# Sequence states read over four 32-column blocks, 96 places for the token tile, and quarters of the first weights, in a decoder trunk on one core

## The chip, the core and the metric

The kernel runs on one core of one Trainium2 chip. The metric is the device time of one execution in microseconds; the median of several runs is compared. One execution is also profiled, and its own time stands beside its span. A core has a matrix engine (TensorE, PE in the rows, with its weight loads as PEld), three engines for elementwise work (VectorE or DVE, ScalarE or ACT, GpSimd or POOL) and a queue that issues DMAs (SyncE or SP).

## The reference

Two layers of a decoder trunk. Each has a feed-forward part, a token mixer and a second feed-forward part. The mixer runs a gated delta rule in four heads (width 128) beside a short gated convolution. Two groups of tokens share the weights: one prompt (16 meta tokens and 256 tokens) and eight sequences of eight sampled tokens, each with a stored 128x128 state per head. What the change touches:

```python
def gdn_chunks(q, k, v, beta, g, s0, chunk):
    ...
    def step(s, inp):
        qd, kt, uc, wc, qkc, el = inp
        nv = uc - jnp.einsum('bhlk,bhkv->bhlv', wc, s)
        o = jnp.einsum('bhlk,bhkv->bhlv', qd, s) + jnp.einsum('bhij,bhjv->bhiv', qkc, nv)
        s = el[..., None, None] * s + jnp.einsum('bhlk,bhlv->bhkv', kt, nv)
        return s, o
```

For the eight sequences there is one chunk of eight tokens. So each sequence and head needs its stored state `s0` multiplied with its eight q columns (for `o`) and its eight k columns (for `nv`). The mean-square norms, the convolutions and the projections are as in any such trunk. Inputs and outputs are fp32.

## The kernel before

**Layout.** Features lie on the 128 partitions, tokens in the free dimension: 256 prompt tokens, then 64 sampled and 16 meta tokens, 336 in all (320 at the end, where the meta tokens are no longer needed). The mixer works on three token tiles; tiles 0 and 1 are the prompt's, tile 2 (`C_TILE`) holds the 64 sampled and the 16 meta tokens, 80 of its 128 places.

**Large products.** Weights come as fp32 in chunks of 512 KB halves (slots `RAW0` to `RAW2`), two halves to a chunk in the feed-forward entry: gate and up. ScalarE rounds a half to `WH`, VectorE makes the rest `WL = RAW - WH` in place; activations are split in the same way into `XH` and `XL`. One product of a tile is then three matmuls (`WH XH`, `WH XL`, `WL XH`) of 128x128 by 336.

**Start.** `entry` of layer 0 first runs 14 warm-up matmuls on zeros, then gate for the input tiles kt 0 to 3, up for the same, both for kt 4 to 7, and then the second chunk's two tiles one after the other. The SP queue issues x and the halves in the order that the rows of the change's section show.

**Mixer.** A hand-written list `BEHIND_PART` says which small steps stand behind each third of an input projection tile (`part`, six to nine large matmuls). All engines walk through the same list, each doing its piece of a step and waiting on semaphores for the pieces of others. Steps named in `EVACUATED_BY` are numbered; each writes one of three PSUM banks (5 + number mod 3) in turn, and `bank_free` on TensorE waits until the step three before has been read out. The steps near the change: `qk`, `kk` (products of keys with queries and keys), `unit`, `nt`, `x`, `y`, `mirror` (a triangular inverse by doubling, in 32x32 blocks, on MB, NB, XM and EGB), `vt`, `kt` (transposes of values and keys), `kst` (transpose of the keys times states), `nv`, `st`, `oC`, `o`, `o_cols`, `rob` (the recurrence's products and the output's norm).

**Reads.** `read` steps 0 to 7 (line 1912) multiply the stored states: per head and sequence the 128x128 state is the stationary side, and 16 columns, eight of q and eight of k, move. Four such matmuls make a step. The result stands in bank 3 (`READ_QK`), with features on the partitions; after read 7 ScalarE copies the k part to `KST`, which `kst` turns.

## Time and profile before

| | us |
|---|---|
| median of 3 runs | 1404.74 (1404.52 to 1405.12) |
| profiled execution | 1401.58 |
| its span | 1399.8 |
| TensorE busy | 1379.2 (99%) |
| VectorE busy | 860.7 (61%) |
| ScalarE busy | 638.7 (46%) |
| GpSimd busy | 30.8 (2%) |
| mean granted TensorE clock | 0.995 of full |

The page's sections give busy time by engine, the span in 40 slices, the DMA queues, the chain that ended last, and the costliest groups. In the rows further down, a line of the time order has the start in us, the length in us, engine, line, operation, output<-inputs, the size of the stationary side (rows\*columns) for TensorE, the size of the moving side, and a count; in square brackets the idle time before it and what ended it. An fp32 matmul shows as two records. A record's length runs to the end of its result, so the pace of a queue is read from start to start.

### The profile page before, as it was taken

Reading aid. Unit: us, or ns where it says so; the run is one execution under the profiler, and the core shown is the slowest. Engines: PE = TensorE matmul, PEld = TensorE weight load, DVE = VectorE, ACT = ScalarE, POOL = GpSimd, SP = SyncE. Lnnn points to the kernel's source line nnn. Section 1 sums busy time; section 2 is a strip of 40 time slices with the busy share of each in tenths; the row PEclk is TensorE's granted clock in tenths of the full one; section 3 lists DMA queues with packets and bytes.
Section 4 is the critical chain, followed back from the end, with each engine's and each line's share of the span. In section 5 each row is a group of like instructions: output and inputs, shape, how many; then the busy total and the mean of one; then the engine's idle time right before and its main releaser. Section 6 shows DMA issues by size and latency. Waiting matters only on the chain.

```text
span 1399.8 us, 25130 instructions
## 1 busy us (share of the span) xinstructions
PE 1379.2 (99%) x10704; PEld 1355.8 (97%) x10704; DVE 860.7 (61%) x1527; ACT 638.7 (46%) x1021; POOL 30.8 (2%) x129
## 2 busy tenths in 40 slices
PE   9999999999999999999999999999999999999997
PEld 9999999989999999999999999999899999999997
DVE  5655533798696765553376555337976968555433
ACT  5433333583635543433354443336826355444331
POOL 0000000110000000000000000001100000000000
PEclk9999999999999999999999999999999999999998
DMA  6644344422125344434435443444221263444342
GB/s 211 221 151 138 117 143 145 149 93 93 67 77 203 121 151 144 133 121 146 164 131 194 144 150 123 144 138 139 91 98 61 91 219 121 151 151 151 125 145 100
DMA packets 49760, 190.93 MB, mean 136 GB/s; under 512 B 6160, under 2 KB 8720, under 8 KB 49136
## 3 DMA queue, kind: packets, MB, share of 16 engines
q1 hardware_dynamic: 49040, 184.19, 39.1%
q0 software_dynamic: 608, 5.12, 0.9%
q8 instruction: 85, 1.39, 0.4%
q14 instruction: 27, 0.22, 0.0%
HBM read 182.86 MB, written 6.43 MB: 135 GB/s over the span
## 4 chain that ended last, share of the span: by engine, by line
PE 92%; DVE 4%; ACT 3%; issue 1%; DMA 0%; SPq 0%; ACTq 0%
PE PS L1552 26%; PE PS L1553 26%; PE PS L1554 26%; PE PS L1592 2%; PE PS L1597 2%; PE PS L1593 2%; PE PS L1758 2%; DVE WL L1077 1%; PE PS L1912 1%; DVE CV L1239 1%; PE PS L1756 1%; PE PS L1887 1%; PE PS L1868 0%; PE PS L1979 0%; ACT WH L746 0%
## 5 line engine op out<-in xcount | busy, mean ns | idle before, releaser
L1552 PE MATMUL PS<-XH,WH 128*128 128x336 f32 (+1 forms) x1728 | 549.8, 318 | 0.3 <-DVE WL L1077 0.3
L1554 PE MATMUL PS<-XH,WL 128*128 128x336 f32 (+1 forms) x1728 | 542.9, 314 | 0.0
L1553 PE MATMUL PS<-XL,WH 128*128 128x336 f32 (+1 forms) x1728 | 542.6, 314 | 0.0
L1077 DVE TENSOR_TENSOR WL<-RAW,WH 128x1024 fp32r<-128x1024 f32 (+1 forms) x312 | 398.7, 1301 | 193.7 <-ACT WH L746 193.3
L746 ACT ACTIVATE WH<-RAW 128x1024 fp32r<-128x1024 f32 (+1 forms) x312 | 343.9, 1120 | 226.9 <-DMA RAW<-in_w_down 170.9
L1552 PEld LDWEIGHTS PS<-XH,WH 128*128 128x128 f32 x1728 | 325.1, 188 | 4.2 <-issue 3.1
L1553 PEld LDWEIGHTS PS<-XL,WH 128*128 128x128 f32 x1728 | 325.2, 188 | 0.4
L1554 PEld LDWEIGHTS PS<-XH,WL 128*128 128x128 f32 x1728 | 324.9, 188 | 0.0
L1552 PE MATMUL PS<-HH,WH 128*128 128x336 f32 (+1 forms) x704 | 221.4, 314 | 0.0
L1553 PE MATMUL PS<-HL,WH 128*128 128x336 f32 (+1 forms) x704 | 221.3, 314 | 0.0
L1554 PE MATMUL PS<-HH,WL 128*128 128x336 f32 (+1 forms) x704 | 221.2, 314 | 0.0
L1201 DVE TENSOR_TENSOR GR<-PS,RB 128x336 f32<-128x336 f32 (+1 forms) x88 | 44.2, 503 | 186.4 <-PE PS L1554 186.3
L841 ACT ACTIVATE HH<-HF 128x336 fp32r<-128x336 f32 (+1 forms) x88 | 42.6, 484 | 203.1 <-DVE HF L1209 203.1
L1552 PEld LDWEIGHTS PS<-HH,WH 128*128 128x128 f32 x704 | 132.6, 188 | 0.0
L1553 PEld LDWEIGHTS PS<-HL,WH 128*128 128x128 f32 x704 | 132.2, 188 | 0.0
L1554 PEld LDWEIGHTS PS<-HH,WL 128*128 128x128 f32 x704 | 132.1, 188 | 0.0
L839 ACT ACTIVATE SG<-GR 128x336 f32<-128x336 f32 (+1 forms) x88 | 42.4, 482 | 114.5 <-DVE GR L1201 114.5
L1211 DVE TENSOR_TENSOR HL<-HF,HH 128x336 fp32r<-128x336 f32 (+1 forms) x88 | 44.4, 505 | 48.4 <-ACT HH L841 48.4
L1592 PE MATMUL PS<-XH,WH 128*128 128x336 f32 (+1 forms) x177 | 57.1, 326 | 1.9 <-DVE WL L1077 1.9
L1593 PE MATMUL PS<-XH,WL 128*128 128x336 f32 (+1 forms) x177 | 55.6, 318 | 0.0
L1239 DVE SCALAR_TENSOR_TENSOR CV<-EXT,PAR_ALL,CV 128x360 f32<-128x360 f32 x72 | 42.6, 591 | 4.9 <-ACT CV L876 3.2
L1597 PE MATMUL PS<-XL,WH 128*128 128x336 f32 (+1 forms) x177 | 45.3, 319 | 0.0
(283 smaller groups left out, 1222.0 us busy)
## 6 DMA issues: line engine op xcount, KB each, us to landing
RAW<-in_w_up SPq DMA_DIRECT2D x176, 512.0 KB, 4.3
RAW<-in_w_down SPq DMA_DIRECT2D x64, 704.0 KB, 4.1
RAW<-in_w_in SPq DMA_DIRECT2D x56, 512.0 KB, 4.4
RAW<-in_w_out SPq DMA_DIRECT2D x16, 512.0 KB, 4.4
SEQ_S<-in_states SPq DMA_DIRECT2D x2, 2048.0 KB, 10.7
out_state_s<-SEQ_S POOLq DMA_DIRECT2D x2, 2048.0 KB, 8.9
X<-in_x SPq DMA_DIRECT2D x8, 168.0 KB, 5.1
out_y<-X SPq DMA_DIRECT2D x4, 320.0 KB, 2.3
```

The source lines that it names most:

```text
L746: act.activation(WH[slot][:, cols], RAW[slot][:, cols], ACT.Copy).then_inc(split_hi.sem, 1)
L841: act.activation(hidden(HH, c, n), HF[k][:, 0:n], ACT.Copy).then_inc(h_hi.sem, 1)
L1077: dve.tensor_tensor(WL[slot][:, cols], RAW[slot][:, cols], WH[slot][:, cols].bitcast(F32), ALU.subtract).then_inc(split_lo.sem, 1)
L1201: dve.tensor_tensor(GR[k][:, 0:n], PS[:, up_bank(c, 0), 0:n], RB[:, 0:n], ALU.mult).then_inc(gate_scaled.sem, 1)
L1211: dve.tensor_tensor(hidden(HL, c, n), HF[k][:, 0:n], hidden(HH, c, n).bitcast(F32), ALU.subtract).then_inc(h_lo.sem, 1)
L1239: ins = dve.scalar_tensor_tensor(cv, src[:, n, tap:tap + length - taps + 1], PAR_ALL[:, layer, col:col + 1], cv, ALU.mult, ALU.add)
L1552: pe.matmul(out, wh, xh, start=first, stop=False)
L1553: pe.matmul(out, wh, xl, start=False, stop=False)
L1554: return pe.matmul(out, wl, xh, start=False, stop=last)
L1592: pe.matmul(out, wh, XH[:, kt, 0:n], start=(kt == 0), stop=False)
L1593: pe.matmul(out, wl, XH[:, kt, 0:n], start=False, stop=False)
L1597: ins = pe.matmul(out, wh, XL[:, kt, 0:n], start=False, stop=(kt == KT - 1))
```

## The change

Three edits.

1. **Reads.** The eight `read` steps of a layer go. GpSimd blanks a new tile `QKZ` (it shares its place with `TMP`) and, at step `qk` of tile 2, copies q and k of each sequence into it, in pairs of sequences with 16 zero columns between them. A new step `tread`, numbered and read out by ScalarE into `VS`, runs 32 matmuls: stationary side a window of 32 columns of `QKZ` (one sequence's 16 columns and 16 zeros), moving side the 128 columns of the state, output one of four 32-column blocks of the array. The two sequences of a pair add up in one block. One later step `read` multiplies the result with a 0/1 matrix `seq_order`, which puts it into `READ_QK` as before. VectorE's step for projection tiles c waits for the copy, since `TMP` shares its place with `QKZ`.
2. **96 places.** Steps of tile 2 work on 96 instead of 128 places (`C_SPAN`), `kst` on 64: fewer columns, and three instead of four 32x32 blocks.
3. **Quarters.** At the very start the first two chunks are loaded and split in quarters of 512 columns. The first quarters of all four tiles come first, and `entry` runs kt 0 to 3 of gate, up, gate2, up2, then kt 4 to 7 of gate and up, then of gate2 and up2. The squares of x on ScalarE stand behind all splits of these chunks.

```diff
+C_SPAN = 96
...
+PAIR_W = 6 * SEQ_T
...
-    [("read", 0), ("x", 0, 2), ("y", 2, 2), ("silu", 9)],
-    [("lo", 5, 1), ("mirror", 2, 2), ("read", 1), ("conv", 10), ("nt", 1), ("x", 2, 4)],
+    [("x", 0, 2), ("y", 2, 2), ("silu", 9)],
+    [("lo", 5, 1), ("mirror", 2, 2), ("conv", 10), ("nt", 1), ("x", 2, 4), ("tread",)],
...
+        tmp_at = region(max(2 * T, HEADS * SEQS // 2 * PAIR_W) * 4)
+        (TMP0, TMP1), _ = stack(tmp_at, ("TMP0", [P, T], F32), ("TMP1", [P, T], F32))
+        (QKZ,), _ = stack(tmp_at, ("QKZ", [P, HEADS, SEQS // 2, PAIR_W], F32))
+        TMP = [TMP0, TMP1]
...
+        def span_of(t):
+
+            return C_SPAN if t == C_TILE else P
+
+        def own_cols(t):
+
+            return slice(t * P, t * P + span_of(t))
...
+        def quarters(half):
+
+            return [slice(half * A_LEN // 2 + q * A_LEN // 4, half * A_LEN // 2 + (q + 1) * A_LEN // 4) for q in range(2)]
...
+            def load_quarter(c, half, q):
+
+                cols = quarters(half)[q]
+                ready = early_in[c][half] if q == 0 else raw_in[c][half].sem
+                sp.dma_start(RAW[c][:, cols], source(0, c)[:, cols]).then_inc(ready, 16)
+
             load_x(0)
-            load_half(0, 0, 0)
+            load_quarter(0, 0, 0)
             for m in range(1, 4):
                 load_x(m)
-            load_half(0, 0, 1)
-            for m in range(4, KT):
-                load_x(m)
-            load(0, 1)
+            load_quarter(0, 1, 0)
+            load_quarter(1, 0, 0)
+            load_quarter(1, 1, 0)
+            load_x(4)
+            load_x(5)
+            load_quarter(0, 0, 1)
+            load_quarter(0, 1, 1)
+            load_x(6)
+            load_x(7)
+            load_quarter(1, 0, 1)
+            load_quarter(1, 1, 1)
...
+                pool.memset(QKZ[:, :, :, :], 0.0).then_inc(qk_blank.sem, 1)
...
+                    elif what == "qk" and t == C_TILE:
+
+                        pool.wait_ge(q_decayed.sem, q_decayed.at(ORDER.index(C_TILE), layer))
+                        pool.wait_ge(qk_blank.sem, qk_blank.at(0, layer))
+                        for h in range(HEADS):
+                            for k in range(2):
+                                own = QKV[:, h + HEADS * k, N_PROMPT:N_PROMPT + N_SAMPLE].rearrange(
+                                    "p (a b i) -> p a b i", b=2, i=SEQ_T)
+                                for b in range(2):
+                                    at = 4 * SEQ_T * b + SEQ_T * k
+                                    ins = pool.tensor_copy(QKZ[:, h, :, at:at + SEQ_T], own[:, :, b, :])
+                        ins.then_inc(qk_spread.sem, 1)
...
-                    elif what == "read" and t == READS - 1:
+                    elif what == "tread":
+
+                        evacuated(act.activation(VS[:, C_TILE, :, :], group(step, layer), ACT.Copy))
+                    elif what == "read":
...
+                    act_group(("tread",), layer)
...
-                        dve.tensor_tensor(qT(tcols(t)), qT(tcols(t)), QKM[:, t, :, :], ALU.mult).then_inc(q_decayed.sem, 1)
+                        own_t, s = own_cols(t), span_of(t)
+                        dve.tensor_tensor(qT(own_t), qT(own_t), QKM[:, t, :, 0:s], ALU.mult).then_inc(q_decayed.sem, 1)
                         dve.wait_ge(q_decayed.sem, q_decayed.at(NTH[step], layer))
                         dve.wait_ge(dd_exp.sem, dd_exp.at(NTH[step], layer))
-                        evacuated(dve.tensor_tensor(QKM[:, t, :, :], group(step, layer), DA[:, t, :, :], ALU.mult))
+                        evacuated(dve.tensor_tensor(QKM[0:s, t, :, 0:s], group(step, layer)[0:s, :, 0:s], DA[0:s, t, :, 0:s],
+                                                    ALU.mult))
...
+            def early_low(n):
+
+                c, cols = n // 2, quarters(n % 2)[0]
+                dve.wait_ge(early_hi, n + 1)
+                dve.tensor_tensor(WL[c][:, cols], RAW[c][:, cols], WH[c][:, cols].bitcast(F32),
+                                  ALU.subtract).then_inc(early_lo, 1)
+
+            def rest_low(c, half):
+
+                cols = quarters(half)[1]
+                dve.wait_ge(split_hi.sem, split_hi.at(PIECE[c] + half, 0))
+                dve.tensor_tensor(WL[c][:, cols], RAW[c][:, cols], WH[c][:, cols].bitcast(F32),
+                                  ALU.subtract).then_inc(split_lo.sem, 1)
+
             prenorm(0, 0, 0)
-            split_low(0, 0, 0)
+            early_low(0)
             for m in range(1, 4):
                 prenorm(0, 0, m)
-            split_low(0, 0, 1)
-            for m in range(4, KT):
-                prenorm(0, 0, m)
-            split_low(0, 1, 0)
-            split_low(0, 1, 1)
+            for n in range(1, 4):
+                early_low(n)
+            prenorm(0, 0, 4)
+            prenorm(0, 0, 5)
+            rest_low(0, 0)
+            rest_low(0, 1)
+            prenorm(0, 0, 6)
+            prenorm(0, 0, 7)
+            rest_low(1, 0)
+            rest_low(1, 1)
...
-                    for kt in range(4):
-                        part(kt, gate)
+                    for n_early, tile in enumerate((gate, up, gate2, up2)):
+                        pe.wait_ge(early_lo, n_early + 1)
+                        for kt in range(4):
+                            part(kt, tile)
+                    split(layer, at, 0)
                     split(layer, at, 1)
-                    for kt in range(4):
-                        part(kt, up)
                     for kt in range(4, KT):
                         part(kt, gate, up)
-                    for tile in (gate2, up2):
-                        split(layer, at + 1, tile[1])
-                        for kt in range(KT):
-                            part(kt, tile)
+                    split(layer, at + 1, 0)
+                    split(layer, at + 1, 1)
+                    for kt in range(4, KT):
+                        part(kt, gate2, up2)
                     return
+                split(layer, at, 0)
...
-            def per_head_products(name, layer, lhsT, rhs, transpose=False):
+            def per_head_products(name, layer, lhsT, rhs, transpose=False, rows=P, cols=P):
                 bank_free(name, layer)
-                out = heads_bank(name)
+                out = heads_bank(name)[0:rows, :, 0:cols]
                 for h in range(HEADS):
                     if transpose:
-                        ins = pe.transpose(out[:, h, :], lhsT(h), mask("ident"))
+                        ins = pe.transpose(out[:, h, :], lhsT(h), mask("ident", cols)[0:cols])
...
-                                for b in range(P // SQUARE):
+                                for b in range(span_of(t) // SQUARE):
...
+                    elif what == "tread":
+
+                        pe.wait_ge(states_in.sem, states_in.at(0, layer))
+                        pe.wait_ge(qk_spread.sem, qk_spread.at(0, layer))
+                        bank_free(step, layer)
+                        out = heads_bank(step)
+                        for h in range(HEADS):
+                            for b in range(2):
+                                for pair in range(SEQS // 2):
+                                    window = QKZ[:, h, pair, 2 * SEQ_T * b:2 * SEQ_T * b + QUAD]
+                                    ins = pe.matmul(out[block(pair), h, :], window, SEQ_S[:, 2 * pair + b, h, :],
+                                                    start=(b == 0), stop=(b == 1))
+                        ins.then_inc(filled.sem, 1)
                     elif what == "read":
 
-                        h, half = t // 2, t % 2
-                        if t == 0:
-                            pe.wait_ge(states_in.sem, states_in.at(0, layer))
-
-                            pe.wait_ge(proj_read.sem, proj_read.at(3, layer))
-                            pe.wait_ge(q_decayed.sem, q_decayed.at(ORDER.index(C_TILE), layer))
-                        for s in range(half * SEQS // 2, (half + 1) * SEQS // 2):
-                            own = slice(s * SEQ_T, (s + 1) * SEQ_T)
-                            cols = slice(N_PROMPT + s * SEQ_T, N_PROMPT + (s + 1) * SEQ_T)
-                            ins = pe.matmul(READ_QK[:, h, :, own], SEQ_S[:, s, h, :], QKV[:, h:2 * HEADS:HEADS, cols],
-                                            start=(h == 0 and s == 0), stop=(h == HEADS - 1 and s == SEQS - 1))
-                        if t == READS - 1:
-                            ins.then_inc(seq_read.sem, 1)
+                        pe.wait_ge(proj_read.sem, proj_read.at(3, layer))
+                        evacuated(("tread",), layer)
+                        for h in range(HEADS):
+                            ins = pe.matmul(READ_QK[:, h, :, :], VS[:, C_TILE, h, :], mask("seq_order"), start=(h == 0), stop=(h == HEADS - 1))
+                        ins.then_inc(seq_read.sem, 1)
...
+    found["seq_order"] = (col % N_SAMPLE // SEQ_T == row // (2 * SEQ_T)) & (col // N_SAMPLE == row // SEQ_T % 2) & (col % SEQ_T == row % SEQ_T)
```

The same edit of `C_SPAN` is made in the other steps of tile 2.

TensorE around the first two reads, layer 0, before. NB, XM, EGB and MB are the inverse's tiles; L1552 to L1554 are the large matmuls:

```order
1965 L1554 MATMUL PS<-XH,WL_57 128x336
1966 L1912 MATMUL PS<-QKV,SEQ_S 128x2x8 x4
1967 L1868 MATMUL PS<-NB_110,DA 32x16 x16
1968 L1887 MATMUL PS<-EGB,MB_117 32x16 x16
1969 L1552 MATMUL PS<-XH,WH_58 128x336
...
1977 L1554 MATMUL PS<-XH,WL_55 128x336
1978 L1912 MATMUL PS<-QKV,SEQ_S 128x2x8 x4
1979 L1868 MATMUL PS<-NB_116,DA 32x16 x16
1980 L1552 MATMUL PS<-XH,WH_58 128x336
...
1988 L1554 MATMUL PS<-XH,WL_55 128x336
1989 L1887 MATMUL PS<-XM_79,MB_111 32x16 x16
1990 L1887 MATMUL PS<-EGB,MB_117 32x16 x16
```

And after (L1646 to L1648 are the large matmuls, L2008 is `tread`):

```order
1963 L1648 MATMUL PS<-XH,WL_57 128x336
1964 L1965 MATMUL PS<-NB_111,DA 32x16 x16
1965 L1984 MATMUL PS<-EGB,MB_118 32x16 x12
1966 L1646 MATMUL PS<-XH,WH_58 128x336
...
1974 L1648 MATMUL PS<-XH,WL_55 128x336
1975 L1965 MATMUL PS<-NB_117,DA 32x16 x12
1976 L2008 MATMUL PS<-SEQ_S,QKZ 32x128 x32
1977 L1646 MATMUL PS<-XH,WH_58 128x336
...
1985 L1648 MATMUL PS<-XH,WL_55 128x336
1986 L1984 MATMUL PS<-XM_79,MB_112 32x16 x16
1987 L1984 MATMUL PS<-EGB,MB_118 32x16 x12
```

Two reads of four matmuls went, the 32 matmuls of `tread` stand behind the third x step, and x and y of tile 2 have 12 matmuls. The order products (four of 128x128) stand where reads 3 and 4 stood.

The SP queue at the start, before (RAW_52 and RAW_53 are the first two chunks):

```order
1 L632 DMA PAR_ALL<-in_par 128x218
2 L630 DMA X<-in_x 128x336
3 L612 DMA RAW_52<-in_w_up 128x1024
4 L630 DMA X<-in_x 128x336 x3
5 L612 DMA RAW_52<-in_w_up 128x1024
6 L630 DMA X<-in_x 128x336 x4
7 L612 DMA RAW_53<-in_w_up 128x1024 x2
8 L641 DMA MK<-in_masks 128x256
```

After:

```order
1 L650 DMA PAR_ALL<-in_par 128x218
2 L648 DMA X<-in_x 128x336
3 L655 DMA RAW_52<-in_w_up 128x512
4 L648 DMA X<-in_x 128x336 x3
5 L655 DMA RAW_52<-in_w_up 128x512
6 L655 DMA RAW_53<-in_w_up 128x512 x2
7 L648 DMA X<-in_x 128x336 x2
8 L655 DMA RAW_52<-in_w_up 128x512 x2
9 L648 DMA X<-in_x 128x336 x2
10 L655 DMA RAW_53<-in_w_up 128x512 x2
11 L672 DMA MK<-in_masks 128x256
```

The first quarters of both chunks now stand ahead of x 4 to 7.

ScalarE at the start, before (L771 makes XH, L746 WH, L775 the squares):

```order
2 L771 ACTIVATE XH<-X,PAR_ALL 128x336
3 L746 ACTIVATE WH_58<-RAW_52 128x1024
4 L771 ACTIVATE XH<-X,PAR_ALL 128x336 x3
5 L746 ACTIVATE WH_58<-RAW_52 128x1024
6 L771 ACTIVATE XH<-X,PAR_ALL 128x336 x4
7 L775 ACTIVATE SQ_122<-X 128x336 x4
8 L746 ACTIVATE WH_59<-RAW_53 128x1024 x2
9 L775 ACTIVATE SQ_122<-X 128x336 x4
10 L746 ACTIVATE WH_60<-RAW_54 128x1024 x2
```

After:

```order
2 L815 ACTIVATE XH<-X,PAR_ALL 128x336
3 L1089 ACTIVATE WH_58<-RAW_52 128x512
4 L815 ACTIVATE XH<-X,PAR_ALL 128x336 x3
5 L1089 ACTIVATE WH_58<-RAW_52 128x512
6 L1089 ACTIVATE WH_59<-RAW_53 128x512 x2
7 L815 ACTIVATE XH<-X,PAR_ALL 128x336 x2
8 L1095 ACTIVATE WH_58<-RAW_52 128x512 x2
9 L815 ACTIVATE XH<-X,PAR_ALL 128x336 x2
10 L1095 ACTIVATE WH_59<-RAW_53 128x512 x2
11 L819 ACTIVATE SQ_123<-X 128x336 x8
```

Eight roundings of 512 columns stand in place of four of 1024, and all squares behind them.

## Rows read from the trace of the kernel before

**Rows 1.** Busy time by engine, from the page's first section.
```profile
PE 1379.2 (99%) x10704; PEld 1355.8 (97%) x10704; DVE 860.7 (61%) x1527; ACT 638.7 (46%) x1021; POOL 30.8 (2%) x129
```

**Rows 2.** The reads: their group (count, busy us, mean ns), then time order.
```profile
L1912 PE MATMUL PS<-QKV,SEQ_S 128*128 128x16 f32 x128 | 15.4, 255 | 0.0
...
330.79 0.96 PE L1912 MATMUL PS<-QKV,SEQ_S 128*128 128x16 f32 x8
331.68 0.44 PE L1868 MATMUL PS<-NB,DA 32*32 32x16 f32 x32
```

**Rows 3.** Time order, TensorE: small products over four blocks, and one weight load.
```profile
312.80 0.48 PE L1797 MATMUL PS<-SQX,MK 128*32 128x336 f32 x2
312.81 0.48 PE L1797 MATMUL PS<-SQY,MK 128*32 128x336 f32 x2
313.50 0.42 PE L1552 MATMUL PS<-XH,WH 128*128 128x336 f32 x1
...
312.84 0.12 PEld L1797 LDWEIGHTS PS<-SQY,MK 128*32 128x32 f32 x2
...
367.74 1.08 PE L1943 MATMUL PS<-VS,MB 32*32 32x128 f32 x32
368.75 0.42 PE L1552 MATMUL PS<-XH,WH 128*128 128x336 f32 x1
```

**Rows 4.** Time order, TensorE: eight products, x and y steps, transposes of keys.
```profile
315.32 1.95 PE L1758 MATMUL PS<-QKV 128*128 128x128 f32 x16
317.03 0.40 PE L1552 MATMUL PS<-XH,WH 128*128 128x336 f32 x1
...
335.72 0.44 PE L1868 MATMUL PS<-NB,DA 32*32 32x16 f32 x32
335.99 0.96 PE L1887 MATMUL PS<-XM,MB 32*32 32x16 f32 x64
...
364.38 0.60 PE L1756 MATMUL PS<-MK,KST 128*128 128x128 f32 x4
364.91 0.68 PE L1861 MATMUL PS<-N,DA 64*64 64x64 f32 x8
```

**Rows 5.** Time order of GpSimd, VectorE and ScalarE around the reads.
```profile
256.17 2.00 POOL L690 COPY EXT<-HIST_G 128x24 f32<-128x24 f32 x12
277.86 1.52 POOL L704 COPY NEW_G<-EXT 128x3 f32<-128x3 f32 x1 [7.30 <-DVE EXT L1260]
...
312.01 0.69 DVE L1363 TENSOR_TENSOR QKV<-QKV,QKM 128x512 f32<-128x512 f32 x1 [1.07 <-PE PS L1758]
...
329.81 0.21 DVE L1417 TENSOR_TENSOR NB<-NB,PS 128x64 f32<-128x64 f32 x1
...
333.14 0.42 ACT L894 ACTIVATE QKV<-CV 128x256 f32<-128x256 f32 x1 [16.30 <-DVE CV L1239]
```

**Rows 6.** Start in time order, then windows (busy of PE, PEld, DVE, ACT, POOL, PEclk).
```profile
1.07 6.04 PE L2016 MATMUL PS<-TMP 128*128 128x128 f32 x28 [1.07 <-DVE TMP L1515]
8.97 0.42 PE L1592 MATMUL PS<-XH,WH 128*128 128x336 f32 x1 [1.86 <-DVE WL L1077]
...
24.36 0.32 PE L1597 MATMUL PS<-XL,WH 128*128 128x336 f32 x1
25.43 0.32 PE L1552 MATMUL PS<-XH,WH 128*128 128x336 f32 x1
...
4.41 0.58 ACT L771 ACTIVATE XH<-X,PAR_ALL 128x336 fp32r<-128x336 f32 x1 [2.38 <-DMA X<-in_x]
6.60 1.06 ACT L746 ACTIVATE WH<-RAW 128x1024 fp32r<-128x1024 f32 x1 [1.61 <-DMA RAW<-in_w_up]
...
9.22 1.06 ACT L746 ACTIVATE WH<-RAW 128x1024 fp32r<-128x1024 f32 x1 [0.16 <-DMA RAW<-in_w_up]
...
10.00:12.00 2.00, 2.00 (x9) 1.78 (x8) 2.00 (x4) 2.00 (x5) 0.00 (x0) 0.52 1.05 385
...
376.00:378.00 2.00, 2.00 (x9) 2.00 (x8) 1.94 (x3) 1.98 (x3) 0.00 (x0) 0.50 0.00 0
```

133 lines of the change are left out of this document (78 added, 55 removed).

## The prediction

> **What bounds the kernel now.** I read the page first, then the matmul groups by form, then the order of time on TensorE, then VectorE, ScalarE and GpSimd at the same places. The page gives TensorE 1379.2 busy of 1399.8 us, 99%, against 61% for the next engine [rows 1]. The kernel's time is what stands in TensorE's queue, plus what it waits. So an edit is worth the time between the start of the removed instructions and the start of the next one. The two mixers hold the sequence reads: 128 records of 15.4 us together (two records are one fp32 matmul) [rows 2]. A read step of four matmuls stands at 330.79, and the next instruction at 331.68: 0.89 us for only 16 moving columns each [rows 2]. Four 128-column products cost nearly the same, eight of them 1.71 us [rows 4]. So a read is paid for its 128x128 stationary state, not for the columns that move. The profiled execution took 1401.58 us (span 1399.8), 3.2 us under the median of the timed runs, 1404.74. I take differences from the trace and subtract them from the median.
>
> **Reads (edit 1).** Removed per layer: 8 steps at 0.89, 7.1 us. Added per layer: 32 products with 32 stationary and 128 moving columns over four column blocks, two rounds of four per head, 8 rounds; then four 128x128 order products. Two rows come near to a round. Four products with 32 stationary columns, one in each block, with 336 moving ones, stand at 312.80 to 312.81, and the next instruction at 313.50: 0.70 us, so four run side by side; scaled to 128 columns 0.27. Sixteen 32x32 tiles with 128 moving columns go from 367.74 to 368.75, four rounds in 1.01, 0.25 each [rows 3]. Both carry a turn into the next instruction of about 0.1 us once. Eight rounds are then between 8 x 0.21 + 0.1 = 1.8 and 8 x 0.27 = 2.2; I take 1.9, nearer the second row, which has several rounds in a row as here. If the four blocks didn't share time, each product would cost what one of the eight in 1.71 us does, 0.21, and 32 of them 6.8 us: the far bound, against the 0.70 row. The order products are half of 1.71, 0.86 us [rows 4]. Three times a small step followed a read directly and now pays the turn itself, 0.2 us per layer together. Net: 7.1 - 1.9 - 0.86 - 0.2 = 4.15 per layer, **8.3 us** in all.
>
> A rule bears on the round. In the first of these two rows the last of the eight weight loads starts at 312.84, while the products of the first pass run [rows 3]. The Trainium skill, "TensorE: Matmul & The Clock Gate", section "The mechanism", says that a weight load overlaps a running matmul only where its row group is another one; all four column blocks share all rows. By that rule the loads would stand between the rounds; it is the first rival below. The 0.70 us row doesn't show such a gap, but holds only two passes.
>
> **What has to be ready for them.** GpSimd copies q and k into the padded tile, 16 small copies, after the decay of q at 312.01 (0.69 us). Like copies took 2.00 us for 12, 0.17 each [rows 5]: done by 315.5. The 32 products are due near 330.3 (the x step at 331.68, its 0.28, less the two reads ahead). Cover: 15 us. Behind these copies on GpSimd stand only history copies whose results leave by DMA at the end of the stage; the new memset of 768 elements goes into the seven us before 277.86 in which the engine waits [rows 5]. The 128x512 copy out of PSUM falls to ScalarE, whose queue then stands idle for 16.30 us until 333.14 [rows 5]; a copy of about 0.6 us from 332.2 is gone before that, and the x step that needs the bank comes two steps and one part later, near 334.2. The keys are copied to KST four parts earlier than now. Nothing here is on the path.
>
> What gets tighter is the x step behind the first y step. Its operand leaves VectorE at 329.81 to 330.02 [rows 5] and is used at 331.68 now; without the two reads it would be used near 330.0. VectorE gets some shorter operations ahead of it (96 instead of 128). From then on the 32 products (1.9) stand where two reads (1.8) stood, so the next ones keep their distance. Later each group loses 0.9 us at most against gaps of VectorE of 0.4 to 1 us. I charge **0.5 us** for such waits in all, bounds 0 and 2.
>
> **96 places (edit 2).** On TensorE per layer: qk and kk of the token tile, 8 products of 0.21 (1.71 / 8), go from 128 to 96 on both sides. Between nothing (a record costs 0.11 with 16 moving columns too) and a quarter, 0.43; I take 0.35, since here the stationary side shrinks too. Six x and y steps lose 4 of 16 small products; such a step is 0.27 (335.72 to 335.99) [rows 4], a quarter is 0.07: 0.4. nv keeps its four rounds, nothing. The rest 0.1. Together 0.85 per layer, **1.7 us**, bounds 0 and 2.2. Shorter operations on VectorE and ScalarE lie beside TensorE.
>
> The turned keys now fill 64 rows. Today four transposes take 0.53 us (364.38 to 364.91), under the 0.86 of four products [rows 4]. The Trainium skill, "TensorEngine Tiling (Array Packing)", section "Restrictions", says that column tiling switches off the transpose mode for fp32. If that befell this step, it would cost 0.3 us per layer more, 0.7 in all. No row shows a transpose of 64 columns, so I don't count it.
>
> **Quarters at the start (edit 3).** Now: x lands and is read at 4.41, the first half of the weights at 6.60, ScalarE takes 1.06, VectorE the 1.2 up to TensorE's start at 8.97; its warm-up products had ended at 7.11, an idle of 1.86 us. Then its granted clock falls: 0.52 of full speed in 10 to 12 us, nearly all of it at the lower level, 1.2 GHz. The entry ends at 25.43; the seven products before that take 1.07, 0.153 each [rows 6]. Ninety-six of them are 14.7, so 1.7 us of the 16.46 are the clock's and the turn's. New: the first quarter is 0.26 MB earlier in the queue than the half was. From 0.28 MB at 4.4 and 0.80 MB at 6.6 it lands at 5.5. ScalarE and VectorE need about 0.6 and 0.7 on 512 columns: ready at 6.9, and TensorE starts at 7.05, right behind its warm-up. Gate takes 12 products, to 9.0. The up quarter closes 1.32 MB; with 1.85 MB at 9.22 [rows 6] it lands at 7.9, and is split at about 9.4: a wait of 0.4. The other two are ready by 11, the second quarters by 13 to 15 against needs at 15 and 18.6. Then 84 products end at 22.4. Chunk 2 is split later than before (the squares now stand ahead of it, to about 20.4 on VectorE), but still before 22.4. That is 25.43 - 22.4 = **3.0 us**, 1.9 of it the earlier start and the rest the clock. Bounds: 0.5 (quarters that land late, clock still low) and 3.6.
>
> **Sum.** 8.3 + 1.7 + 3.0 - 0.5 = 12.5 us. 1404.74 - 12.5 = **1392.2**; the profiled execution would be near 1389.1, its span 1387.3.
>
> **Rivals.**
> *Loads between rounds.* Each of the 16 passes of a layer (8 rounds, two passes) waits for four loads of 32 columns. Four reads with eight 128-column loads took 0.89, 0.11 a load, so four of 32 columns are again 0.11: 16 x 0.11 = 1.7 per layer, 3.4 in all: 1395.6. For it: the blocks share rows. Against: 0.70 for two passes of 336.
> *The start gives nothing.* 2 KB pieces move more slowly, or the wait for the up quarter lets the clock fall all the same: 1395.2. For it: a gap of 1.86 did it. Against: the queue order, and that the new gap is 0.4.
> *The clock in the mixer.* Layer 0 has a stretch at the lower level (0.50 at 376 to 378 [rows 6]) behind a row of small-tile steps, of about the start's price, 1.7 us; layer 1 has none. With fewer busy tiles there may be none, one or two: -1.7 or +1.7 on the forecast.
> *The change doesn't do what it says.* The four blocks run one after another: reads 7.1 against 6.8 + 0.86: 8.3 turns into -1.5: 1402.
> *Slower: GpSimd's copies.* They decide from 1.1 us each (17.6 us from 312.7 to 330.3 over 16). One small copy there took 1.52 us [rows 5]. At that price 16 take 24.3 us: TensorE stands 6.7 us in each layer, and a gap over 1.86 us brings a low-clock stretch of 1.7: 2 x 8.4 = 16.8 on top: 1409. Against: that copy was the first of its line after a long rest, and twelve others took 0.17 each.
>
> **Chances.** Forecast with its clock variants 0.67, loads between rounds 0.12, no gain at the start 0.12, no sharing 0.04, copies 0.04, the rest 0.01. A measurement of this kernel can tell about 0.2%, 2.8 us, from no change. Faster by more 0.93, within 0.03, slower 0.04. Range: low end 1389.0 (forecast, start and 96 at their better bounds and no low clock in the mixer), high end 1397.5 (either of the first two rivals with a low-clock stretch more).
>
> **What would show it.** Right: the 32 products span under 2 us, the order products 0.86; TensorE's idle before its first product near 0.1, the granted clock 1.00 from 10 to 14 us, chunk 2's first product near 22.4; no wait of TensorE on GpSimd or on the bank. Wrong: 3.4 or 6.8 us for the 32 products, a clock of 0.5 before 20 us, or idle time before the third x step.

## The result

| | before | after |
|---|---|---|
| median of the first comparison, us | 1404.63 (1403.46 to 1405.12, 4 runs) | 1388.07 (1386.85 to 1390.4, 4 runs) |
| profiled execution, its span | 1401.58, 1399.8 | 1390.4, 1388.6 |
| all executions measured here, median | 1400.91 (1398.44 to 1406.25, 74, without the first series) | 1388.25 (1386.85 to 1391.13, 15, with the first series) |

The ratio of the first comparison is 0.9885, 95% interval 0.9868 to 0.9902: 16.6 us less, where 12.5 was forecast. The time lies 0.9 us below the range. Two later series of the same kernel, beside before on the same chip, gave 0.9911 (0.9896 to 0.9926) and 0.9908 (0.9892 to 0.9924), 12.4 and 12.7 us.

Busy time by engine, after, as in [rows 1]:

```profile
PE 1369.5 (99%) x10608; PEld 1344.1 (97%) x10608; DVE 859.2 (62%) x1529; ACT 638.6 (46%) x1027; POOL 38.1 (3%) x163
```

TensorE is busy 9.7 us less. Time order of TensorE after (start, length, engine, line, operation, count of records). The rows show, from the top, the first large product, the one that waits for up, chunk 2's first product, the token tile's products, the reads, the order products and the turned keys.

```profile
6.47 0.40 PE L1686 MATMUL PS<-XH,WH 128*128 128x336 f32 x1
...
9.41 0.42 PE L1686 MATMUL PS<-XH,WH 128*128 128x336 f32 x1 [0.46 <-DVE WL L1602]
...
22.40 0.32 PE L1646 MATMUL PS<-XH,WH 128*128 128x336 f32 x1
...
312.04 1.76 PE L1853 MATMUL PS<-QKV 128*96 128x96 f32 x16
313.55 0.40 PE L1646 MATMUL PS<-XH,WH 128*128 128x336 f32 x1
...
326.96 1.95 PE L2008 MATMUL PS<-SEQ_S,QKZ 128*32 128x128 f32 x64
328.85 0.42 PE L1646 MATMUL PS<-XH,WH 128*128 128x336 f32 x1
...
347.23 1.05 PE L2016 MATMUL PS<-MK,VS 128*128 128x128 f32 x8
348.21 0.44 PE L1961 MATMUL PS<-NB,DA 32*32 32x32 f32 x16
...
357.27 0.60 PE L1851 MATMUL PS<-MK,KST 128*64 128x128 f32 x4
357.80 0.68 PE L1958 MATMUL PS<-N,DA 64*64 64x64 f32 x8
```

The 32 read products take 1.89 us, the order products 0.98, eight products of 96 columns 1.51 (1.71 in [rows 4]), the keys 0.53 as in [rows 4]. Chunk 2 begins at 22.40, where before needed until 25.43 [rows 6].

GpSimd and ScalarE at the same places, after. The copies into QKZ (2.94 us for 16, 0.18 each) and the copy out of PSUM are long done when they are needed:

```profile
267.45 0.74 POOL L727 MEMSET QKZ<- 128x768 f32 x1
...
309.33 2.94 POOL L760 COPY QKZ<-QKV 128x32 f32<-128x32 f32 x16 [0.55 <-DVE QKV L1427]
...
328.98 0.60 ACT L1048 ACTIVATE VS<-PS 128x512 f32<-128x512 f32 x1 [15.43 <-PE PS L2008]
```

Three windows of after (from:to, busy us and counts of PE, PEld, DVE, ACT, POOL, granted clock of TensorE, DMA share, GB/s), to set beside the two in [rows 6]:

```profile
10.00:12.00 2.00, 2.00 (x15) 2.00 (x15) 1.92 (x4) 1.95 (x5) 0.00 (x0) 1.00 1.06 395
368.00:370.00 2.00, 2.00 (x13) 1.94 (x9) 1.77 (x3) 2.00 (x4) 0.00 (x0) 0.50 0.03 8
1061.00:1063.00 2.00, 2.00 (x9) 2.00 (x8) 1.94 (x3) 1.78 (x3) 0.00 (x0) 0.50 0.00 0
```

The clock is full at the start now. But there are two stretches at 1.2 GHz in the mixers, from 367.6 to 371.0 and from 1060.5 to 1063.9, each about 3.4 us at half speed, 1.7 us lost. Before had two as well, one at the start and one at 375. They are not in every execution: the changed kernel's second profile (a_again below) has neither, and took 1387.46 us instead of 1390.4. Its third (a_again2) has both at the same places, from 368.6 and 1061.5, and took 1391.04. Here are the two windows in a_again:

```profile
368.00:370.00 2.00, 2.00 (x27) 1.92 (x27) 1.84 (x5) 1.85 (x4) 0.00 (x0) 1.00 0.03 10
1061.00:1063.00 2.00, 2.00 (x20) 1.84 (x19) 1.94 (x4) 1.27 (x5) 0.00 (x0) 1.00 0.00 0
```

The table below sorts the 74 executions of before, taken in four series beside the experiments, by mean granted clock, with the changed kernel's 15:

| mean granted clock | before: count, lowest, median, highest | after: count, times |
|---|---|---|
| 0.997 | 24: 1398.44, 1399.24, 1400.37 | 6: 1386.85 to 1387.83 |
| 0.996 | 11: 1399.95, 1400.97, 1402.06 | 5: 1387.94 to 1389.14 |
| 0.995 | 16: 1400.34, 1400.98, 1402.06 | 4: 1389.03 to 1391.13 |
| 0.994 | 14: 1402.53, 1403.1, 1403.99 | none |
| 0.991, 0.992 | 9: 1403.41 to 1406.25 | none |

At 0.997 the two differ by 1399.24 - 1387.42 (the median of six) = 11.8 us. The medians of all differ by 12.7. The four executions of before in the first comparison lie where later series have clocks of 0.994 or less; their own clocks weren't recorded. The record names chips 2, 4, 6 and 12 for the four later series and none for the first. At 0.997 before's median is 1399.10, 1399.36, 1399.44 and 1399.16 us on these four, so times of different series can be compared at equal clock to about 0.3 us.

### The profile page after: what moved, and what is told of

It is laid out like the page before. It is cut to its first block, busy times and chain, and to the rows that moved or that the text cites. A ratio compares the mean times of both kernels' runs of the same rounds, so it can differ in the third digit from the quotient of the medians.

```text
span 1388.6 us, 24998 instructions
## 1 busy us (share of the span) xinstructions
PE 1369.5 (99%) x10608; PEld 1344.1 (97%) x10608; DVE 859.2 (62%) x1529; ACT 638.6 (46%) x1027; POOL 38.1 (3%) x163
## 3 DMA queue, kind: packets, MB, share of 16 engines
q8 instruction: 84, 1.38, 0.4%
## 4 chain that ended last, share of the span: by engine, by line
PE 91%; DVE 4%; ACT 3%; issue 1%; DMA 0%; SPq 0%; ACTq 0%; DVEq 0%
PE PS L1646 26%; PE PS L1647 26%; PE PS L1648 26%; PE PS L1686 2%; PE PS L1691 2%; PE PS L1687 2%; PE PS L1853 2%; DVE WL L1139 1%; DVE CV L1301 1%; PE PS L1851 1%; PE PS L1965 1%; PE PS L1984 0%; PE PS L1702 0%; DMA RAW<-in_w_up 0%; ACT VS L954 0%
## 5 line engine op out<-in xcount | busy, mean ns | idle before, releaser
L1646 PE MATMUL PS<-XH,WH 128*128 128x336 f32 (+1 forms) x1728 | 550.2, 318 | 0.2 <-DVE WL L1139 0.2
L1648 PE MATMUL PS<-XH,WL 128*128 128x336 f32 (+1 forms) x1728 | 543.5, 315 | 0.3 <-issue 0.3
L1139 DVE TENSOR_TENSOR WL<-RAW,WH 128x1024 fp32r<-128x1024 f32 (+1 forms) x308 | 393.5, 1301 | 192.9 <-ACT WH L790 192.5
L790 ACT ACTIVATE WH<-RAW 128x1024 fp32r<-128x1024 f32 (+1 forms) x308 | 339.0, 1120 | 217.1 <-DMA RAW<-in_w_down 171.3
L1646 PEld LDWEIGHTS PS<-XH,WH 128*128 128x128 f32 x1728 | 325.5, 188 | 4.5 <-issue 3.3
L1648 PEld LDWEIGHTS PS<-XH,WL 128*128 128x128 f32 x1728 | 325.4, 188 | 0.5 <-issue 0.5
L1646 PE MATMUL PS<-HH,WH 128*128 128x336 f32 (+1 forms) x704 | 221.4, 314 | 0.0
L1648 PE MATMUL PS<-HH,WL 128*128 128x336 f32 (+1 forms) x704 | 221.1, 314 | 0.0
L1646 PEld LDWEIGHTS PS<-HH,WH 128*128 128x128 f32 x704 | 132.5, 188 | 0.0
L1648 PEld LDWEIGHTS PS<-HH,WL 128*128 128x128 f32 x704 | 132.1, 188 | 0.0
```

Source lines behind the costliest of these rows:

```text
L790: act.activation(WH[slot][:, cols], RAW[slot][:, cols], ACT.Copy).then_inc(split_hi.sem, 1)
L1139: dve.tensor_tensor(WL[slot][:, cols], RAW[slot][:, cols], WH[slot][:, cols].bitcast(F32), ALU.subtract).then_inc(split_lo.sem, 1)
L1646: pe.matmul(out, wh, xh, start=first, stop=False)
L1648: return pe.matmul(out, wl, xh, start=False, stop=last)
```

## Experiments

The line names L... are those of each kernel's own file. "At 0.997" means executions with this mean granted clock.

### The edits apart

**u_reads**: after with the eight reads of before.

```diff
-    [("lo", 5, 1), ("mirror", 2, 2), ("conv", 10), ("nt", 1), ("x", 2, 4), ("tread",)],
+    [("lo", 5, 1), ("mirror", 2, 2), ("read", 1), ("conv", 10), ("nt", 1), ("x", 2, 4)],
...
-                                    ins = pe.matmul(out[block(pair), h, :], window, SEQ_S[:, 2 * pair + b, h, :],
-                                                    start=(b == 0), stop=(b == 1))
+                            ins = pe.matmul(READ_QK[:, h, :, own], SEQ_S[:, s, h, :], QKV[:, h:2 * HEADS:HEADS, cols],
+                                            start=(h == 0 and s == 0), stop=(h == HEADS - 1 and s == SEQS - 1))
```

> The changed kernel with the eight read steps of before put back; 96 places and quarters stay. Theory A (parts as in the prediction, and low-clock stretches that differ from run to run): without low-clock stretches it is 8.3 us slower than the changed kernel, and runs of one kernel differ by steps of about 1.7 us that go with their granted clock; median 1395 to 1399. Theory B (the reads are worth more than their time in TensorE's queue, 4 us more, at the same clock): 12 us slower in every run, near 1400, and the clock of the runs does not go with their times.

Measured: 1396.16 us (1394.1 to 1398.64, 8 runs), 0.9969 of before (0.9958 to 0.998). At 0.997: 1394.1 and 1394.74, 7.0 over the changed kernel, and the times go with the clock. That is the first theory with a smaller size (8.3 expected), and not the 12 of the second.

**u_span**: after with `C_SPAN = 128`.

```diff
-C_SPAN = 96
+C_SPAN = 128
```

> The changed kernel with 128 places for the token tile again (kst stays at 64). Theory A: 1.7 us slower without low-clock stretches, 1389 to 1391. Theory B' (the places are what was undersized): 4 to 6 us slower, 1393.

Measured: 1392.97 us (1391.79 to 1394.35, 5 runs), 0.9946 (0.9933 to 0.9958). At 0.997: 1391.79 and 1392.58, 4.8 over the changed kernel: more than the 1.7 forecast, and more than its upper bound of 2.2. The second theory's price came out; what it consists of is read from the rows further down.

**u_start**: after with the start of before (halves, and x 4 to 7 ahead of the second chunk).

```diff
-            load_quarter(0, 0, 0)
+            load_half(0, 0, 0)
...
-                    for n_early, tile in enumerate((gate, up, gate2, up2)):
-                        pe.wait_ge(early_lo, n_early + 1)
-                        for kt in range(4):
-                            part(kt, tile)
+                    for kt in range(4):
+                        part(kt, gate)
```

> The changed kernel with the start of before (halves). Theory A: the first product of chunk 2 stands near 25.4 instead of 22.4, 3.0 us slower, with a low-clock stretch at 10 to 13.4 in every run: 1390 to 1392. Theory C (the start was undersized: in most timed runs of before the clock stays low longer than in the profiled one): 5 us or more slower.

Measured: 1390.04 us (1390.01 to 1390.48, 4 runs), 0.9925 (0.9912 to 0.9937). That is 1.8 over the changed kernel, where the first theory had 3.0 (its range, 1390 to 1392, was met). Its profile shows the gap of before at the start, but no stretch at half speed behind it, though one was expected in every run. Instead TensorE waits for the second half's remainder, and chunk 2 begins at 24.40, not at 25.43:

```profile
8.10 0.42 PE L1639 MATMUL PS<-XH,WH 128*128 128x336 f32 x1 [1.68 <-DVE WL L1111]
...
11.40 0.42 PE L1639 MATMUL PS<-XH,WH 128*128 128x336 f32 x1 [1.19 <-DVE WL L1111]
...
24.40 0.32 PE L1599 MATMUL PS<-XH,WH 128*128 128x336 f32 x1
```

**o_start**: before with the quarters alone (the edit above the other way round).

> The kernel before with the quarters at the start alone. Theory A: 3.0 us faster than before, near 1401.6, its runs spread by low-clock stretches in the mixer. Theory C: 5 us or more faster, 1399.

Measured: 1399.21 us (1396.89 to 1400.84, 11 runs), 0.9986 (0.9977 to 0.9995), 1.5 us under before's median of that series, 1400.72: half of the 3.0 expected. None of the 11 is below a clock of 0.995; before had 5 of 19.

**o_span**: before with the 96 places alone (`C_SPAN = 96` with old reads and old start).

> The kernel before with the 96 places alone (reads and start of before). In the kernel with the new reads and 128 places, executions at a clock of 0.997 were 4.9 us over those of the changed one: 2.3 us of it shorter products, 2.1 us waits in which TensorE waits for no other engine. Theory (those waits come from too many TensorE instructions in too short a time, and the old reads, 16 records in 0.9 us, gave room): here 96 places are worth the shorter products alone, 1.9 to 2.8 us at equal clock, that is 1395.7 to 1396.8 at 0.997 against before's 1398.5. Additive (96 places are worth the same in any surroundings): 4.4 to 5, 1393.5 to 1394.1.

Measured: 1399.09 us (1395.89 to 1404.19, 12 runs), 0.9984 (0.9972 to 0.9996). At 0.997: 1395.89 and 1396.63, 3.1 under before's 1399.36 of that series; between the medians it is 2.0. The first theory said 1.9 to 2.8, the additive one 4.4 to 5.

Most of the spread of a run stays out if one reads the distance from the first qk step of one mixer to that of the other: a layer's mixer, two feed-forward parts, no start, no end. Before, o_span, u_reads, u_span and a_again, in this order:

```profile
310.82 2.05 PE L1758 MATMUL PS<-QKV 128*128 128x128 f32 x16 [1.05 <-ACT QKV L896]
...
1008.02 2.05 PE L1758 MATMUL PS<-QKV 128*128 128x128 f32 x16 [1.28 <-ACT QKV L896]
```
```profile
309.82 1.84 PE L1789 MATMUL PS<-QKV 128*96 128x96 f32 x16 [1.03 <-ACT QKV L915]
...
1004.36 1.84 PE L1789 MATMUL PS<-QKV 128*96 128x96 f32 x16 [1.25 <-ACT QKV L915]
```
```profile
307.85 1.84 PE L1837 MATMUL PS<-QKV 128*96 128x96 f32 x16 [1.03 <-ACT QKV L928]
...
1002.95 1.84 PE L1837 MATMUL PS<-QKV 128*96 128x96 f32 x16 [1.26 <-ACT QKV L928]
```
```profile
307.80 2.05 PE L1853 MATMUL PS<-QKV 128*128 128x128 f32 x16 [1.03 <-ACT QKV L940]
...
1003.50 2.05 PE L1853 MATMUL PS<-QKV 128*128 128x128 f32 x16 [1.26 <-ACT QKV L940]
```
```profile
308.10 1.84 PE L1853 MATMUL PS<-QKV 128*96 128x96 f32 x16 [1.03 <-ACT QKV L940]
...
999.43 1.84 PE L1853 MATMUL PS<-QKV 128*96 128x96 f32 x16 [1.26 <-ACT QKV L940]
```

| kernel | distance | less 1.7 per half-speed stretch | less waits without a releaser |
|---|---|---|---|
| before | 697.20 | 695.50 | 695.50 |
| o_span | 694.54 | 694.54 | 694.54 |
| u_reads | 695.10 | 695.10 | 694.62 |
| u_span | 695.70 | 694.00 | 691.75 |
| a_again | 691.33 | 691.33 | 690.97 |
| after | 692.65 | 690.95 | 690.56 |
| a_again2 | 692.92 | 691.22 | 690.59 |
| o_start (mixer of before) | 695.38 | 695.38 | 695.38 |
| o_warm (mixer of before) | 695.64 | 695.64 | 695.64 |

The same mixer in several executions differs by up to 0.4 us in the last column, so the terms are known to about that. Within it the edits add up: 96 places are 0.8 to 1.1 us per layer with the old reads and 0.8 to 1.2 with the new ones, the reads 3.65 to 4.06 with 96 places and 3.6 to 3.9 with 128. What doesn't add up are the half-speed stretches and the waits without a releaser: u_span has 0.18 + 1.38 + 0.69 = 2.25 us of the latter in this layer and 3.6 in all; a_again has 0.4.

### The waits without a releaser

The waits of u_span in layer 0 (the last bracket gives the idle time and what ended it; "issue" is nothing that the profile shows):

```profile
331.71 0.30 PE L1984 MATMUL PS<-EGB,MB 32*32 32x16 f32 x13 [0.18 <-issue]
...
335.84 0.42 PE L1984 MATMUL PS<-XM,MB 32*32 32x16 f32 x21 [1.38 <-issue]
...
339.00 0.88 PE L1965 MATMUL PS<-NB,DA 32*32 32x16 f32 x64
...
344.80 0.33 PE L1965 MATMUL PS<-NB,DA 32*32 32x16 f32 x17 [0.69 <-issue]
```

They stand in the middle of steps, at no operand's first use. From the first to the second there are 126 matmul records, from the second to the third 252.

**s_shift**: u_span with 16 one-column products behind the warm-up, 32 records more.

```diff
+            for _ in range(16):
+                pe.matmul(PS[:, 7, 0:1], TMP[0][:, 0:P], TMP[0][:, 0:1], start=True, stop=True)
```

> The changed kernel with 128 places and 16 one-column products (32 records) more behind the warm-up, which cost about 2 to 3.5 us and do nothing. With 128 places TensorE stood idle without any releaser after 51 of 64 records of the first double y step (0.18 us), after 43 of 64 records of the next such y step (1.38) and after 15 of 32 records of an x step at 344.80 (0.69): 126 and 252 records apart. Theory (TensorE waits for its next block of instructions, 126 records with their weight loads): such waits, where there are any, stand 32 records earlier in the program, so after 19 of 64, 11 of 64, and in the y step of 32 records ahead of that x step, or a multiple of 126 records from there. Rival (the operands or banks of these steps): the waits stay at the same products of the same steps.

```profile
340.47 0.72 PE L1965 MATMUL PS<-NB,DA 32*32 32x16 f32 x64
...
342.16 0.32 PE L1646 MATMUL PS<-XH,WH 128*128 128x336 f32 x1 [0.96 <-issue]
```

One execution, 1395.52 us. At none of the theory's three places is there a wait, but two stand 126 records ahead of the third and 126 behind it, as the theory allowed. In u_span this place (behind the x step of 64 records) is 21 + 9 + 64 = 94 records behind the wait at 335.84. A block further than that wait would be 126; 32 earlier is 94. The next wait of s_shift, 1.08 us at 351.75, is 252 records on. All profiles agree: with TensorE's matmul records counted from the first one of the program, each of the 32 waits without a releaser (0.17 to 1.38 us, in 15 of the 18 profiles) stands at a number that leaves 97 to 100 when divided by 126. So the waits are tied to the count of records, not to an operand. The likely reason is that TensorE waits for its next block of instructions: 126 matmul records, each with its weight load, are 252 instructions. The profile doesn't show the loading itself. The Trainium skill, "Runtime: NRT & Kernel Launch", section "Instruction fetch mechanics", says that the program is loaded in blocks of 256 instructions, and that this is mostly hidden. The size comes near (252 counted here). Hidden it is where large products run (none of these waits stands outside the mixers), not always where a block of small ones passes in 2.8 us.

**u_tread**: u_span with the reads moved away from the dense rows.

```diff
-    [("lo", 5, 1), ("mirror", 2, 2), ("conv", 10), ("nt", 1), ("x", 2, 4), ("tread",)],
+    [("lo", 5, 1), ("mirror", 2, 2), ("conv", 10), ("nt", 1), ("x", 2, 4)],
...
-    [("tap", 14), ("hi", 8, 1), ("evac", 15)],
+    [("tap", 14), ("hi", 8, 1), ("evac", 15), ("tread",)],
```

> The changed kernel with 128 places and the sequence reads (64 records in 1.9 us) moved behind a part five parts on, where TensorE had no small products. The kernel with 128 places had 3.6 us of waits for nothing seen in the mixers of its profile, all within 20 us of the reads, and took 1391.8 to 1392.6 at a clock of 0.997. Theory (waits for the next 126 records, when two or three such blocks pass in 3 to 4 us each): without the reads in the dense stretch the waits shrink to 1 us or less, and executions at 0.997 take 1389.5 to 1390.8. Rival (they come with the steps of 128 places wherever the reads are): 2.5 to 3.6 us of waits, 1391.5 to 1392.8.

Measured: 1395.38 us (1395.13 to 1396.89, 5 runs), 0.9952 (0.994 to 0.9965): 2.4 us slower than u_span, not faster, and outside what both theories had. The waits for blocks shrink only to 1.8 us, and a new one comes in each layer, this one with a releaser:

```profile
328.68 0.44 PE L1984 MATMUL PS<-XM,MB 32*32 32x16 f32 x32
330.13 0.44 PE L1984 MATMUL PS<-EGB,MB 32*32 32x16 f32 x32 [1.01 <-DVE EGB L1475]
```

A stretch at half speed from 332 to 339 follows it. The reads, which are ready early, cover VectorE's chain from the x step to the next y step. Their place is not free.

**b_both**: the same move in a_spread (below).

> The kernel a_spread with the sequence reads moved in the same way. Theory: a_spread's waits of 0.2 to 0.4 us for instructions go, its low stretches stay away: 1385 to 1386.5, within 0.5 us of a_spread (1386.23), all executions at 0.997 or above. Rival (a long row of small products behind the moved reads lets the clock fall, or the copy out of PSUM on ScalarE comes late for the order products): 1387 or more, with a wait ahead of the order products or a stretch at 1.2 GHz after 345.

Measured: 1389.87 us (1388.74 to 1393.86, 4 runs), 0.9907 (0.9892 to 0.9922), 3.6 us over a_spread. In the profiled execution, the slowest of the four, VectorE's EGB comes 0.76 and 0.94 us late, and the clock is at half from 1023 to 1037 behind the second. The time is the rival's, but neither the wait nor the place of the stretch is the one that it named.

### Side by side

**a_order**: after with the loops exchanged, so that the two products of one column block follow one another.

```diff
-                            for b in range(2):
-                                for pair in range(SEQS // 2):
+                            for pair in range(SEQS // 2):
+                                for b in range(2):
```

> The changed kernel with the two loops of the sequence reads exchanged: the two products of a column block follow one another, where in the changed kernel four different blocks follow one another. Theory (products in different column blocks run side by side only when they stand next to each other in the queue): the 64 records take 2.8 to 4.5 us instead of 1.89, and the execution 2 to 5 us more. Rival (loads and products flow at the rate of the queue in any order, 0.03 us a record): 1.9 us again, no change.

```profile
326.50 2.03 PE L2008 MATMUL PS<-SEQ_S,QKZ 128*32 128x128 f32 x64
328.45 0.42 PE L1646 MATMUL PS<-XH,WH 128*128 128x336 f32 x1
```

1.95 us against 1.89, and 1387.97 us in its one execution: no change. The order within the 32 products is of no account here; 0.03 us a record in either. The weight loads of the reads stand beside the products and not between them, as the row of the changed kernel shows (its products: 326.96 to 328.85):

```profile
326.96 1.69 PEld L2008 LDWEIGHTS PS<-SEQ_S,QKZ 128*32 128x32 f32 x64
```

### The same kernel again, and before's spread

**a_again** and **a_again2**: the changed kernel, unchanged.

> The changed kernel again, beside kernels of this chip. Theory (times of one kernel go with its number of stretches at 1.2 GHz, 1.7 us each, and the median of before of the first comparison held more of them than the profiled execution): executions with a mean granted clock of 0.997 take 1386.8 to 1387.6 us here too, those with 0.995 some 3 us more, and before at 0.997 takes 1398.2 to 1399.2, so the difference at equal clock is 11.2 to 12.2, not 16.6. Rival (the first comparison was of another chip with another level for before): the difference at equal clock is 15 or more, or the time doesn't go with the clock.

> The changed kernel beside a_spread2. Expected 1386.9 to 1391, median 1388.0 to 1388.9, clocks of 0.995 to 0.997. Together with the two earlier series this gives its distribution; before in the same series is expected at 1398.5 to 1405 with a median of 1400.5 to 1402, so 12 to 13.5 us between the medians, not the 16.6 of the first comparison.

Measured: 1388.7 us (1387.46 to 1391.13, 6 runs) beside 1401.09 of before, and 1387.83 (1386.85 to 1391.04, 5 runs) beside 1400.51. At 0.997 the first of the two series gives 1387.46 against 1399.36, 11.9 us, the second 1387.39 against 1399.44, 12.05. The theory held (11.2 to 12.2), not the rival (15 or more).

**o_warm**: before with 22 instead of 14 warm-up products. **o_wide**: 14 of twice the width.

```diff
-            for _ in range(14):
+            for _ in range(22):
```
```diff
-            dve.memset(TMP[0][:, 0:P], 0.0).then_inc(blank_set, 1)
+            dve.memset(TMP[0][:, 0:2 * P], 0.0).then_inc(blank_set, 1)
...
-                pe.matmul(PS[:, 7, 0:P], TMP[0][:, 0:P], TMP[0][:, 0:P], start=True, stop=True)
+                pe.matmul(PS[:, 7, 0:2 * P], TMP[0][:, 0:P], TMP[0][:, 0:2 * P], start=True, stop=True)
```

> The kernel before with 22 instead of 14 warm-up products: TensorE works through the 1.1 to 1.9 us in which it waited for the first weights. In the two comparisons on this chip 10 of 36 executions of before had a clock of 0.994 or less and took 1402.8 to 1405.1 us, against none of the 38 executions of kernels with the quarters at the start. Theory (the gap and the half-speed time behind it make this upper end): no execution at 0.994 or less, median 1399 to 1400, while the lowest stays at 1398.5 to 1399.5, since the first weights land no earlier; no stretch at 1.2 GHz at 10 to 14 us. Rival (the upper end comes from the small products of the mixer): times from 1398.5 to 1405 as before, about three of ten at 0.994 or less.

> The kernel before with its 14 warm-up products twice as wide (256 columns): TensorE works through its gap at the start as it does with 22 products, but the number of records is that of before, where 22 products have 16 records more. Theory (what made the kernel with 22 products slower, 1401.3 at least against 1398.5, is that all later instructions stand 16 records later in blocks of 126, so that waits for a block fall into rows of small products): this one has the lowest time of before or up to 1.1 us less, 1397.4 to 1398.8, and a median of 1400 to 1401. Rival (a busy start itself costs clock or time later): 1401 to 1405, as with 22 products.

**o_pad**: before with four products in a wait of each mixer.

```diff
                     elif what == "qk":
+                        if t == C_TILE:
+                            bank_free(step, layer)
+                            for _ in range(4):
+                                pe.matmul(heads_bank(step)[:, 0, 0:1], mask("ident"), mask("ident")[:, 0:1], start=True, stop=True)
```

> The kernel before with four one-column products (8 records, 0.9 us) in the wait of 1.03 to 1.25 us that stands ahead of the first qk step in each layer. They cost nothing by themselves, but shift the rest of layer 0 by 8 and of layer 1 by 16 records, the latter as in the kernel with 22 warm-up products. Theory (place in the blocks of 126 records decides): layer 1's waits without a releaser, where there are any, stand after 31 of 32 and after 23 of 64 records of the y steps, as in that kernel, not at an x step as in before; lowest time 1399.5 to 1401.5, median 1401.5 to 1404. Rival (place has no effect): waits as in before (an idle of 0.88 us at 1034.8), times as before, lowest 1398.5, median 1401 to 1402.

Measured: o_warm 1403.07 us (1401.31 to 1404.99, 11 runs), 1.0009 (0.9999 to 1.002); o_wide 1402.12 (1400.56 to 1403.1, 11), 1.0006 (0.9996 to 1.0017); o_pad 1402.72 (1400.52 to 1405.26, 12), 1.001 (1.0 to 1.002). The same y step of layer 1 in before, o_wide, o_warm and o_pad:

```profile
1033.12 0.77 PE L1887 MATMUL PS<-XM,MB 32*32 32x16 f32 x39
1034.76 0.39 PE L1887 MATMUL PS<-XM,MB 32*32 32x16 f32 x25 [0.88 <-issue]
```
```profile
1030.83 0.77 PE L1887 MATMUL PS<-XM,MB 32*32 32x16 f32 x39
1032.74 0.39 PE L1887 MATMUL PS<-XM,MB 32*32 32x16 f32 x25 [1.14 <-issue]
```
```profile
1030.67 0.37 PE L1887 MATMUL PS<-XM,MB 32*32 32x16 f32 x23
1032.12 0.60 PE L1887 MATMUL PS<-XM,MB 32*32 32x16 f32 x41 [1.09 <-issue]
```
```profile
1030.81 0.37 PE L1891 MATMUL PS<-XM,MB 32*32 32x16 f32 x23
1032.53 0.60 PE L1891 MATMUL PS<-XM,MB 32*32 32x16 f32 x41 [1.35 <-issue]
```

The place follows the count to the record: after 39 of 64 with before's number of records, after 23 with 16 more. In the last three a stretch at half speed begins 1.3 to 1.5 us behind the end of the wait, at 1033 or 1034, 3.4 us lost. One window of o_warm:

```profile
1034.00:1036.00 2.00, 2.00 (x69) 1.60 (x68) 0.48 (x3) 0.00 (x0) 0.00 (x0) 0.50 0.00 0
```

So a wait for a block among small products and the half speed behind it cost 4 to 5 us together in one execution. In the other profiles 1.38 us (u_span) and 0.88 (o_start) were followed by it; 0.88 in before, 0.91 and 0.87 (u_tread), 0.96 and 1.08 (s_shift) were not. That is five of ten such waits, and the changed kernel has its stretches without one, so it isn't shown that the wait brings the stretch.

The times of o_pad lie where the theory had them (lowest 1399.5 to 1401.5, median 1401.5 to 1404). The others don't: four of o_warm's eleven executions have a clock of 0.994 or less, where none was expected, and its median went the rival's way. o_wide has the waits at before's places and should have had before's lowest times or better; none of its executions is under 1400.56, none of o_warm's or o_pad's under 1400.52, while 18 of the 38 executions of before beside them are. The place of the wait is settled; what lifts the lowest times of these three is not. What the traces show of it stands at the start: the wider warm-up ends so late that the first large product comes at 9.93 (before: 8.97), and the longer one lets it start at 8.36 but then waits 0.88 us for up. Chunk 2 begins at 24.85 in o_wide and 24.34 in o_warm, no earlier than in profiles with the gap and without a stretch (24.40 in u_start, 24.47 in o_span): the weights set this time.

### A better version

**a_spread** and **a_spread2**: after with two small steps moved, so that a row of small products, 3.4 us from 364.6, is broken up.

```diff
-    [("st", 2), ("key_lo", 1), ("evac", 18), ("oC",), ("mirror", 1, 16), ("o", 2), ("x", 1, 32), ("hi", 10, 0), ("lo", 9, 0),
+    [("key_lo", 1), ("evac", 18), ("oC",), ("mirror", 1, 16), ("o", 2), ("hi", 10, 0), ("lo", 9, 0),
      ("val_lo", 0)],
-    [("hi", 10, 1), ("val_twin", 0), ("lo", 9, 1)],
+    [("st", 2), ("x", 1, 32), ("hi", 10, 1), ("val_twin", 0), ("lo", 9, 1)],
```

> The changed kernel with the state step of the token tile (eight records of 16 rows, 1.1 us) and the fifth x step of tile 1 (0.5 us) moved behind the next part. The work is the same. In the changed kernel 3.5 us of small products stand in a row at 364.6 and at 1056.6, and its granted clock falls to half behind each for 3.4 us. Theory (the row of small products lets the clock fall): no low stretch at 367 to 372 nor at 1060 to 1064, mean clock up by 0.001 to 0.002, 1.7 to 3.4 us less than the changed kernel, 1384 to 1386. Rival (the low stretches come without regard to this row): same distribution of times as the changed kernel, 1387 to 1390, and low stretches elsewhere or at the same places.

> a_spread once more: the changed kernel with the token tile's state step and an x step behind the next part. Theory (fewer low stretches behind a shorter row of small products): 1385.5 to 1387 and a clock of 0.997 in nearly all executions, 1.5 to 3 us less than the changed kernel beside it. Rival (its first four executions were a draw): the changed kernel's distribution, 1386.9 to 1391, with 0.995 among them.

Measured: 1386.23 us (1385.58 to 1386.95, 4 runs), 0.9891 of before (0.9875 to 0.9906), and 1386.95 (1386.44 to 1388.16, 4 runs), 0.9903 (0.9887 to 0.9919). All eight executions have a clock of 0.997 or more, against 6 of 15 of the changed kernel, and both profiles are at full clock throughout the mixers, here where after is at half:

```profile
368.00:370.00 2.00, 2.00 (x30) 1.84 (x28) 1.10 (x3) 1.69 (x3) 0.00 (x0) 1.00 0.00 0
1061.00:1063.00 2.00, 2.00 (x19) 1.93 (x17) 1.97 (x4) 1.02 (x5) 0.00 (x0) 1.00 0.00 0
```

The medians differ by 2.5 and 0.9 us in the two series, where 1.5 to 3 was expected of the second. The intervals overlap, so the gain in time is likely, not certain; the clock's part is the clearer one.

## Why the prediction was off

**The base.** This is the step that failed: "subtract them from the median". The sum was made on an execution of 1401.58 us and put under three runs that agreed within 0.6 us at 1404.74. The 74 later executions of before reach from 1398.44 to 1406.25, with a median of 1400.91; the profiled one was near their middle, the three runs at their upper end. From 1400.91 the same sum gives 1388.4, 0.3 off the measured 1388.07. The prediction's other figure, 1389.1 for a profiled execution, is 1.0 off the median of 1388.07 and 1.3 below the profiled 1390.4. Whether all runs of the first series were slow by chance, or by something that the later series didn't have, stays open; the record doesn't name the chip of the first. Of the 74, 8 were at 1403.46 or more, as all four of that series were, and 4 at 1404.5 or more, as three of them were, so chance alone is not likely. The difference of the first comparison, 16.6 us, is too large for the change itself by the later ones: 11.8 us at equal clock, 12.7 between medians.

**The sum, 12.5 us: near, in part by luck.** The terms measured are 7.3 to 8.1 for the reads, 1.6 to 2.4 for the places, 1.5 to 2.0 for the start and nothing for VectorE's waits, 10.4 to 12.5 together. Reads and start were put too high, the 0.5 us taken off for waits went the other way, and the waits for blocks and the spread of the clock, which move the time by several us, were not in the sum.

**The range.** It let only the forecast vary, by one half-speed stretch each way, and before not at all. Both programs vary by several: from 1398.44 to 1406.25 is 7.8 us, more than four stretches of 1.7. So the rival of the clock in the mixer had the right mechanism, but was put on the changed kernel only and sized too small: half of that width is 3.9 us. The ends also don't follow from the terms named for them, which give 1389.4 (1392.2 - 0.6 - 0.5 - 1.7) and 1397.3 (1395.6 + 1.7), not 1389.0 and 1397.5.

**Reads, 8.3 us: mechanism right, slightly high.** Measured 7.3 to 8.1 (3.65 to 4.06 per layer). The round of four blocks is 1.89 / 8 = 0.24 us, as taken. The order products took 0.98 instead of 0.86. The eight reads removed were worth 7.0, not 7.1. That makes 3.9 per layer, inside the measured range. The rival of loads between rounds would have shown 3.6 us for the 64 records. The rule of the Trainium skill behind it ("TensorE: Matmul & The Clock Gate", section "The mechanism") isn't borne out here: there is no gap in either order of the products, and the 64 loads run beside them in 1.69 us.

**96 places, 1.7 us: right for what it counted, and something beside it missed.** The shorter products are 0.8 to 1.2 per layer, 1.6 to 2.4 in all. But with fewer small records came fewer waits for blocks: with the new reads u_span had 3.6 us of them, s_shift 2.6, the changed kernel 0.4 to 1.1; with the old reads the profiles had 0.9 to 1.5 at 128 places and 0 and 0.8 at 96 (o_span, u_reads). These waits make up most of what the same edit is worth beyond the products, 3.1 us on before and 4.8 beside the new reads. The turned keys with 64 columns take 0.53 us as before. The extra 0.7 us that could follow from the Trainium skill, "TensorEngine Tiling (Array Packing)", section "Restrictions", isn't there.

**Start, 3.0 us: the right number for one execution.** Chunk 2 begins at 22.40, to the digit, with no gap and a wait for up of 0.46 (0.4 forecast). The digit is luck: TensorE's first large product came at 6.47 instead of 7.05, and the other two profiles of the changed kernel have chunk 2 at 22.78 and 23.05. Of the 3.0 some 1.0 were the clock's (25.43 against u_start's 24.40), as the prediction had it, but the half-speed stretch behind the gap isn't in every execution: u_start had the gap and no stretch, and then waited 1.19 us for weights instead, which the slow products of before had covered. From there to the qk step it lost 309.72 - 307.75 = 2.0 us, not 3.0. At equal clock the start is worth 1.8 (u_reads against o_span), in medians 1.5 (o_start).

**The tightness, 0.5 us.** It was put at VectorE's chain behind the first y step. TensorE has no such wait there in the changed kernel; the reads stand in the right place to cover it, as u_tread shows by 1.01 us a layer without them. The waits that did come are those at every 126th record, 0.8 us in the profile, and before had 0.88 of them too [its row at 1034.76 above]. The argument on waits rested on rows of layer 0 alone; before's wait stands in layer 1.

**Rivals.** GpSimd's copies cost 0.18 us each and were done 15 us before use. The four blocks do run side by side. The start did give something.

## What to carry to other kernels

Before subtracting a sum from a median, ask how far executions of the same program spread, and how many half-speed stretches the profiled one holds; a narrow set of three runs doesn't show it. Read a difference inside one layer, from one fixed step to the same step of the next layer, less stretches and waits, and the terms of a sum can be held against it to about 0.4 us. Where small products stand close together, count the records as well as the microseconds: at 126 records in 2.8 us TensorE waited up to 1.4 us, most likely for its own instructions, and a ready step such as the reads is worth most where another engine's chain is due next.

## What the runs showed of the hardware

- TensorE has idle times without a releaser, 0.17 to 1.38 us, only at every 126th matmul record or a multiple, and only in the mixers, in or beside rows of small products; not every such place has one. They shift record for record with what is put ahead (39 of 64 to 23 of 64 by 16 records more).
- A half-speed stretch (granted clock 0.50) often begins 0.2 to 1.5 us behind a wait of about 1 us among small products (after five of the ten waits without a releaser of 0.87 us or more), or at the end of 3.4 us of small products in a row; the same program has it in one execution and not in the next (0.50 and 1.00 at 368 to 370). It costs 1.7 us or a multiple: 3.4 us lost in o_start, o_wide, o_warm and o_pad.
- In s_shift 32 records of one column took 3.6 us (7.20 to 10.79), and the granted clock was 0.50 from 10.6 to 14.0.
- 64 records of 128x32 stationary and 128 moving columns take 1.89 us, and 1.95 when neighbours share a column block; their 64 weight loads run beside them in 1.69 us.
- Eight warm-up products more, or wider ones, which filled the gap at the start, made before no faster: 1403.07 and 1402.12 us against 1402.02 and 1400.51 beside them. Chunk 2 began no earlier than with a gap; the rest of the reason stays open.
